# Gated products of the layer boundary moved from VectorE to GpSimd, second row tile ahead of a weight unit

## What is computed

```python
for i in range(DEPTH):                       # 4 layers
    h = rms_norm(x, attn_norm[i])
    o = mixer_i(h)                           # begins with the in projection h @ w_in
    x = x + o @ w_o[i]
    x = x + conv_ffn(rms_norm(x, ffn_norm[i]), ...)
    gate = jax.nn.sigmoid(rms_norm(x, ple_norm[i]) @ w_ple_gate[i])
    x = x + gate * (p[i] @ w_ple_proj[i])
```

## Time and profile before

| | |
|---|---|
| median of three runs | 1415.32 us (1413.1 to 1419.65) |
| profiled execution | 1421.83 us, span 1419.7 us |
| TensorE matmul | 1336.5 us busy (94%) |
| VectorE | 962.4 us (68%) |
| ScalarE | 821.2 us (58%) |
| GpSimd | 422.8 us (30%) |
| mean granted TensorE clock | 0.981 of full |

### The profile page before, as it was taken

How to read it: one execution, slowest core, us unless ns; L and a number is a source line. 1 busy time by engine, 2 the same in 40 slices (tenths; PEclk the granted TensorE clock), 3 DMA queues, 4 the chain that set the end, 5 groups by cost and what they waited for, 6 DMA issues and landing times.

```text
span 1419.7 us, 24524 instructions
## 1 busy us (share of the span) xinstructions
PE 1336.5 (94%) x8340; PEld 1179.5 (83%) x8340; DVE 962.4 (68%) x1449; ACT 821.2 (58%) x1421; POOL 422.8 (30%) x505
## 2 busy tenths in 40 slices
PE   6999999999899999999984899999999999999998
PEld 4777899988777799998863789998877777999886
DVE  4767777745676777774576677776475777777635
ACT  4766666634566666663454656665356676666533
POOL 3442233300274223330037213332004531333200
PEclk9999999999999999999997899999999999999999
DMA  7533555555563455555543055556455334555551
GB/s 278 176 119 108 177 180 187 185 190 167 179 208 128 148 169 178 181 188 193 170 155 112 15 163 173 182 178 201 155 194 170 119 100 169 170 185 182 191 174 60
DMA packets 64022, 232.85 MB, mean 164 GB/s; under 512 B 7280, under 2 KB 7408, under 8 KB 63952
## 3 DMA queue, kind: packets, MB, share of 16 engines
q1 hardware_dynamic: 61056, 221.87, 47.1%
q0 software_dynamic: 2896, 10.05, 2.3%
HBM read 230.84 MB, written 1.05 MB: 163 GB/s over the span
## 4 chain that ended last, share of the span: by engine, by line
PE 69%; DVE 13%; ACT 5%; POOL 4%; issue 4%; DMA 3%; SPq 0%; POOLq 0%; ACTq 0%; DVEq 0%
PE bank L1236 21%; PE bank L1212 15%; PE bank L1213 15%; PE bank L1214 15%; DVE w_lo L699 5%; DMA w_raw<-weights 3%; ACT tok L595 2%; DVE tok L746 2%; ACT w_hi L415 1%; POOL tok L1161 1%; DVE hT_lo L754 1%; ACT tok L436 1%; PE bank L1359 1%; POOL hrstd L1066 1%; DVE hT_lo L975 1%
## 5 line engine op out<-in xcount | busy, mean ns | idle before, releaser
L699 DVE TENSOR_TENSOR w_lo<-w_raw,w_hi 128x1024 fp32r<-128x1024 f32 x418 | 555.5, 1367 | 143.8 <-ACT w_hi L415 142.8
L415 ACT ACTIVATE w_hi<-w_raw 128x1024 fp32r<-128x1024 f32 x418 | 421.2, 1054 | 159.4 <-PE bank L1236 115.9
L1212 PE MATMUL bank<-hT_hi,w_hi 128*128 128x256 f32 x1408 | 398.7, 283 | 5.8 <-DVE hT_lo L754 5.8
L1213 PE MATMUL bank<-hT_lo,w_hi 128*128 128x256 f32 x1408 | 398.4, 283 | 0.0
L1214 PE MATMUL bank<-hT_hi,w_lo 128*128 128x256 f32 x1408 | 398.4, 283 | 0.0
L1212 PEld LDWEIGHTS bank<-hT_hi,w_hi 128*128 128x128 f32 x1408 | 270.3, 192 | 7.4 <-issue 7.4
L1213 PEld LDWEIGHTS bank<-hT_lo,w_hi 128*128 128x128 f32 x1408 | 270.3, 192 | 0.0
L1214 PEld LDWEIGHTS bank<-hT_hi,w_lo 128*128 128x128 f32 x1408 | 270.3, 192 | 0.0
L1198 POOL TENSOR_TENSOR gate_c<-gate_c,up_c 128x256 f32<-128x256 f32 x88 | 105.1, 1195 | 292.5 <-ACT gate_c L674 292.5
L1033 DVE SCALAR_TENSOR_TENSOR gate_c<-bank,conv_sb,gate_c 128x255 f32<-128x255 f32 (+1 forms) x176 | 84.0, 478 | 121.5 <-ACT up_c L670 121.5
L1212 PE MATMUL bank<-w_hi,hT_hi 128*128 128x512 f32 (+1 forms) x336 | 137.9, 410 | 9.0 <-DVE hT_lo L754 5.4
(11 more groups left out here) (136 smaller groups left out, 2051.5 us busy)
## 6 DMA issues: line engine op xcount, KB each, us to landing
w_raw<-weights SPq DMA_DIRECT2D x418, 512.0 KB, 4.2
gain<-gains POOLq DMA_DIRECT2D x11, 512.0 KB, 4.6
rel<-rel_in POOLq DMA_DIRECT2D x8, 256.0 KB, 3.7
x<-x_in SPq DMA_DIRECT2D x2, 512.0 KB, 6.0
p_raw<-p_in POOLq DMA_DIRECT2D x4, 256.0 KB, 5.0
out<-x SPq DMA_DIRECT2D x2, 512.0 KB, 2.6
gain<-gains SPq DMA_DIRECT2D x1, 512.0 KB, 5.9
consts<-consts_in POOLq DMA_DIRECT2D x1, 360.0 KB, 4.4
```

What stands on the lines that cost most here:

```text
L415: nc.scalar.activation(w_hi[:, slot, q * HALF:(q + 1) * HALF], w_raw[:, raw, :], ACT.Copy).then_inc(hi_ready, 1)
L699: nc.vector.tensor_tensor(w_lo[:, slot, cols], w_raw[:, half(q)[0], :], w_hi[:, slot, cols].bitcast(F32), ALU.subtract).then_inc(lo_ready, 1)
L1212: nc.tensor.matmul(out_ap, l_hi, r_hi, start=start, stop=False, skip_group_check=True)
L1213: nc.tensor.matmul(out_ap, l_hi, r_lo, start=False, stop=False, skip_group_check=True)
```

## The change

The products `tok * pp` go from VectorE to GpSimd, which signals `gated` after each of them. GpSimd does the two products of tile 0, the `rstd` of tile 0, the two products of tile 1, the `rstd` of tile 1. VectorE keeps the additions, which wait for `gated`. For tile 1, sigmoids (ScalarE) and additions (VectorE) now stand ahead of the split of unit 2, at the three boundaries only (`n % 3 == 0`). The DMA of `p` and the `rstd` of the boundary move in the text of GpSimd's program from the head of one layer to the end of the one before.

```diff
@@ ScalarE, norm
                 round_hT(n, 0)
+                if before:
+                    before(1)
                 if units[:-2]:
                     split_next(units[-2])
-                if before:
-                    before(1)
                 square(n, 1)
@@ VectorE, add_gated
                 for b in range(2):
                     c = slice(b * 512, (b + 1) * 512)
-                    dve.wait_ge(sg_ready, 4 * L + 2 * t + b + 1)
-                    if t == 0 and b == 0:
-                        dve.wait_ge(pp_first, 2 * (L + 1))
-                        dve.wait_ge(pp_second, 2 * (L + 1))
-                    own.inc(nc.vector.tensor_tensor(tok[:, t, c], tok[:, t, c], pp[:, t, c], ALU.mult))
-                    own.wait()
+                    dve.wait_ge(gated, 4 * L + 2 * t + b + 1)
                     last = nc.vector.tensor_tensor(x[:, t, c], x[:, t, c], tok[:, t, c], ALU.add)
@@ VectorE, norm
                 rest_hT(n, 0)
+                if n % 3 == 0:
+                    add(1)
                 if units[:-2]:
                     split_next(units[-2])
-                add(1)
+                if n % 3:
+                    add(1)
@@ GpSimd
+            def token_rstd(n, t):
+                pool.wait_ge(ssq_ready, 2 * n + t + 1)
+                rsqrt(rstd[:, t:t + 1], ssq[:, t:t + 1], 1, rstd_ready)
+
@@ GpSimd, head of a layer
                 if L:
-                    pool.wait_ge(unit_used, FIRST_GATE[L - 1])
-                    pool.dma_start(p_raw[:], p_in[L]).then_inc(p_landed, 16)
-                    norm_rstd(3 * L)
                     pool.wait_ge(x_ready, 6 * L)
@@ GpSimd, end of a layer
+                if L + 1 < DEPTH:
+                    pool.wait_ge(unit_used, FIRST_GATE[L])
+                    pool.dma_start(p_raw[:], p_in[L + 1]).then_inc(p_landed, 16)
+                pool.wait_ge(pp_first, 2 * (L + 1))
+                pool.wait_ge(pp_second, 2 * (L + 1))
+                for t in range(TT):
+                    for b in range(2):
+                        c = slice(b * 512, (b + 1) * 512)
+                        pool.wait_ge(sg_ready, 4 * L + 2 * t + b + 1)
+                        nc.gpsimd.tensor_tensor(tok[:, t, c], tok[:, t, c], pp[:, t, c], ALU.mult).then_inc(gated, 1)
+                    if L + 1 < DEPTH:
+                        token_rstd(3 * L + 3, t)
```

More of the change, by code:

```diff
@@ L338, in trunk @@
         sg_ready = sem("sg_ready")
+        gated = sem("gated")
         dve_own = sem("dve_own")
@@ L1066, in rsqrt @@
                 nc.gpsimd.tensor_tensor(dst, src, neghalf[:, 0:width], ALU.pow).then_inc(done, 1)
+            def token_rstd(n, t):
+                pool.wait_ge(ssq_ready, 2 * n + t + 1)
+                rsqrt(rstd[:, t:t + 1], ssq[:, t:t + 1], 1, rstd_ready)
             def norm_rstd(n):
                 for t in range(TT):
-                    pool.wait_ge(ssq_ready, 2 * n + t + 1)
-                    rsqrt(rstd[:, t:t + 1], ssq[:, t:t + 1], 1, rstd_ready)
+                    token_rstd(n, t)
             own.inc(nc.gpsimd.memset(neghalf[:], -0.5))
```

## The result

The changed kernel took 1408.09 us (median of six runs, 1407.39 to 1411.53), the kernel before 1415.47 us in the six runs beside it. The ratio is 0.9948, its 95% interval 0.9929 to 0.9967: about 7.4 us faster. The forecast was 1407.5 us. The profiled execution has a span of 1406.0 us.

What follows compares the result with a forecast made beforehand. TensorE multiplies 94% of the span, so only its idle and slow time can be won. Boundaries win 11.4 us, less 1.2 at the end and 2.5 for the clock: 7.7 us off 1415.3, forecast 1407.5 us, range 1401 to 1416.

Steps and rivals of the forecast that it cites:

- A product on GpSimd: Each 128x512 product moved to GpSimd: estimated 1.25 us, between bounds of 0.69 and 2.06 us.
- Tile 0: At each boundary, GpSimd products and an addition held by the second product lengthen tile 0's chain: 1.2 us lost.
- The end: From first product to last addition at the kernel's end nothing runs beside: 1.2 us lost, whole.
- Tile 1 earlier: At the boundaries, tile 1's additions end at 372.95 against 376.41; unit 3 starts at 379.85 in place of 382.19.
- Second boundary: Sliding-window boundary: TensorE idles 1.3 us before tile 1's transposes in place of 4.84; 3.3 us won.
- The clock: TensorE's clock falls behind tile 0's new idle time at one boundary in two, 1.7 us each, 2.5 us in all.
- the length of the idle time: Sign for a clock fall at tile 0: its new 2.0 us idle lies between 1.63 (full clock) and 2.31 (low).
- Sum: Whole kernel: 11.4 us won at boundaries, less 1.2 at the end and 2.5 for the clock, 7.7 us.
- The first boundary: Unit 3 starts 2.35 us earlier and no longer runs partly at half clock (0.7 us): 3.1 us won.
- the third: Third boundary: 2.45 us from an earlier unit 3 and 2.55 for the clock, 5.0 us won.
- The rival of slow products: GpSimd products take 2.06 us each, giving 1425 us; turns to a loss from about 1.6 us; chance 0.08.
- Rival 2: Behind the boundaries, the weight stream or q/k chain gives the gain back: about 1 us won, 1414.5 us; chance 0.10.

Runs made afterwards that it cites:

- experiment 4: Changed kernel with VectorE's additions reading the gate projection's PSUM bank instead of the gated product, so the output omits the gate; one execution took 1407.36 us.
- experiment 1: Kernel before with only tile 1's sigmoids and additions moved ahead of unit 2, products staying on VectorE; 1405.67 us, ratio 0.9917.
- experiment 3: Changed kernel with tile 1's sigmoids and additions back behind unit 2, so only the products move to GpSimd; 1425.09 us against 1418.14, ratio 1.0052.
- experiment 9: Changed kernel with each GpSimd product done as two multiplications, one behind the other; 1430.38 us, ratio 1.0082 to the kernel before.
- experiment 8: Kernel with reordered tile 1, products on VectorE and unit 0's first half split early, plus weight halves moved around tile 1's scaling; 1404.68 us, ratio 0.9914.
- experiment 6: Changed kernel with the rest of tile 0's hT taken ahead of unit 1's split at the boundaries; 1413.79 us, ratio 0.9970 to the kernel before.
- experiment 7: Unit 0's first half split before tile 0's rstd: with only tile 1's order changed 1402.2 us, ratio 0.9899; on the changed kernel 1408.87 us, 0.9941.

## Why the prediction was right

Step by step, by its own terms:

- **A product on GpSimd, 1.25 us:** 1.26 to 1.29 us for all 16 in each of the two traces. Right.
- **Tile 0, +1.2 us, the first addition held:** 3.69 us against 2.74, +0.95, a quarter us less than said; experiment 4 shows the hold. Start of the in projection 13.7 us after the first sigmoid against 12.6, idle 1.9 us where 2.0 was said.
- **The end, +1.2:** +0.9.
- **Tile 1 earlier:** additions end 16.2 us after the first sigmoid, against 19.9; said were 16.4. Unit 3 starts at 22.9 us (third boundary, clock 1.00), said were 23.3. `rstd` met VectorE's split, as said: its first instruction took 0.59, 1.08 and 0.89 us at the three boundaries in place of 0.22, where the sum had a wait of about 0.6. Experiments 1 and 3 show that the order carries all of the gain.
- **Second boundary, 3.3 us:** 3.3 by the means of two traces each. The 1.3 us idle before the transposes did not appear: the low clock had fallen behind tile 0 in both traces, and the slow matmuls lasted until the transposes (723.00), just behind `tok` (722.60); a wait of 1.1 us for tile 1's `hT_lo` came behind.
- **The clock, one boundary in two, 1.7 us each:** the 1.9 us idle had a low clock behind it at two of three boundaries in one trace and at all three in the other. Between the first boundary and the third of the first trace, which had none, it cost 24.44 - 22.87 = 1.57 us. The price was right. The prediction took the length of the idle time as the sign; five falls in six lie above its half, but experiment 3 has the same 1.9 us three times without one, so the length alone does not decide, and what does is open.
- **Sum:** 7.7 us said; 7.4 us by the medians, 8.4 by the cut traces. The first boundary gave 2.2 us, where 3.1 less the clock's 1.7 were said; the third 3.8 of 5.0, with the clock fallen in one trace of two. That forecast and median agree to 0.6 us is in part luck: the tile 0 and end terms were 0.3 us too large each, the clock came oftener than counted, and two traces of one kernel differ by up to 1.9 us in a stretch.

What the prediction did not say is that the change holds a gain and a loss that can be taken apart: the order wins 0.8%, the products on GpSimd lose about 0.25% of it. Its own terms (-1.2 us at each boundary and at the end) say so, and I did not draw the line to the kernel without them. The rival of slow products would have turned at 1.8 to 1.9 us per product by experiment 9 (an estimate, a straight line between -8.4 us at 1.27 and +13.3 at 2.6 to 3.0, the two multiplications of a pair), said were 1.6. Rival 2, a gain given back in the layer behind, did not decide here; in experiment 8 the second stretch took what the first had won.

## What to carry to other kernels

Ask which queue an instruction waits in before asking which engine is less busy: moving tile 1's sigmoids, products and additions ahead of a weight unit won 0.8%; giving the products to an engine with 70% idle time lost a third of it, since they stood on a chain where the neighbour waited anyway. Work given to a second engine is not always beside the first: here an addition beside a product took 1.77 us in place of 0.69. And look for what sets the end of a stage, here unit 3 by tile 1's chain: experiments 6 and 7 closed an idle time ahead of it without unit 3 starting any earlier.

## What the runs showed of the hardware

- Between VectorE's additions and GpSimd's products, both with two SBUF operands, the one that started first ran at its own pace and the other was longer. In the changed kernel the second product starts 0.06 to 0.08 us before the first addition at every boundary, takes 1.28 to 1.29 us, and the addition takes 1.75 to 1.77. In experiment 6 tile 1's first product starts within VectorE's split of unit 1 and takes 2.26 us, so that the pair shows as 3.51.
- A waiting addition can go ahead of GpSimd's next instruction. In experiment 9, where a wait on its own semaphore stands between GpSimd's multiplications, the addition that started at 360.35 waited for a multiplication (360.27 to 361.56) and ended at 362.11; the multiplication behind that one started at 361.64 and was the longer one this time:

```profile
360.35 1.76 DVE L730 TENSOR_TENSOR x<-x,tok 128x512 f32<-128x512 f32 x1 [4.72 <-POOL tok L1216]
361.64 1.62 POOL L1216 TENSOR_TENSOR tok<-tok,pp 128x512 f32<-128x512 f32 x1
```

- VectorE's rest of hT, with one operand in PSUM, ran its 1.28 us beside the products in the changed kernel, unlengthened.
- After idle times of 1.9 us at tile 0 TensorE's granted clock fell behind five of six in the two traces of the changed kernel, and behind none of three in experiment 3's. Behind the 2.25 us of experiment 6 it fell at the first boundary and not at the third. Behind the 1.55 us of experiment 4's trace, and the 0.9 us of the order alone, it did not fall:

```profile
1047.00:1055.00 8.00, 6.44 (x29) 5.01 (x28) 6.92 (x8) 5.01 (x8) 3.14 (x3) 1.00 0.83 264
```

That row is the third boundary of experiment 4.
